# First quarter of the input projection as two parts of 256 rows, behind four condition loads instead of eight

## The reference

```python
mod = (jax.nn.silu(c) @ w_mod[l] + b_mod[l])[:, None, :]           # w_mod: 2048 x 12288
sa, ca, ga, sm, cm, gm = jnp.split(mod, 6, axis=-1)
mod_c = jax.nn.silu(c_ctx) @ w_mod[l] + b_mod[l]
sa_c, ca_c, ga_c, sm_c, cm_c, gm_c = jnp.split(mod_c, 6, axis=-1)
h_c = modulate(x_ctx, norm_attn_w[l], sa_c, ca_c)                  # rmsnorm(x, w) * (1 + scale) + shift
p_c_kv = h_c @ w_in[l][:, K_OFF:P_OFF]                             # keys and values of the context
h = modulate(x, norm_attn_w[l], sa, ca)
p = h @ w_in[l]                                                    # q, k, v, pool input u, gates
```

## Time and profile before

| | before |
|---|---|
| median of 3 runs | 2303.81 us |
| the profiled execution | 2304.4 us |
| its span | 2302.6 us |
| PE busy | 2264.9 us, 98% |
| first matmul of the projection | at 36.38 us |
| first matmul of the second quarter | at 126.13 us |
| DMA mean | 206 GB/s |

### The profile page before, as it was taken

The page is one execution under the profiler, slowest core; times in us unless marked ns, Lnnn a source line. Parts: engine busy times, 40 slices in busy tenths (PEclk is TensorE's granted clock), DMA queues, the critical chain, the costliest instruction groups (busy, mean ns, idle before and its releaser), DMA issues.

```text
span 2302.6 us, 30456 instructions
## 1 busy us (share of the span) xinstructions
PE 2264.9 (98%) x11865; PEld 1857.9 (81%) x11865; DVE 1551.5 (67%) x2297; ACT 1064.1 (46%) x1587; POOL 72.7 (3%) x91
## 2 busy tenths in 40 slices
PE   6999999999999999999999999999999999999998
PEld 3677787777888788888888888888987888899977
DVE  3577798777888776676655555754676545578875
ACT  4343234555544644344444443454554444466654
POOL 1100001110000100000000000000000000000000
PEclk8999999999999999999999999999999999999999
DMA  9999894444689677667655555555434566442233
GB/s 369 300 316 319 289 321 155 139 146 153 231 291 329 206 271 243 222 234 251 229 191 187 189 191 185 171 187 191 147 129 146 183 226 197 148 127 93 93 131 126
DMA packets 235011, 474.82 MB, mean 206 GB/s; under 512 B 7672, under 2 KB 10080, under 8 KB 233872
## 3 DMA queue, kind: packets, MB, share of 16 engines
q1 hardware_dynamic: 231280, 460.35, 59.5%
q0 software_dynamic: 3296, 12.74, 1.9%
q10 hardware_dynamic: 320, 0.13, 0.0%
HBM read 471.10 MB, written 2.10 MB: 206 GB/s over the span
## 4 chain that ended last, share of the span: by engine, by line
PE 96%; DMA 1%; DVE 1%; ACT 1%; issue 1%; SPq 0%; POOLq 0%; POOL 0%
PE acc L1884 75%; PE acc L2304 8%; PE acc L2346 2%; PE aux L2380 2%; PE turn L2360 2%; PE turn L1965 1%; PE aux L1917 1%; PE turn L2101 1%; DMA arena<-in_x 1%; DMA raw<-in_w_mod 1%; PE aux L2492 1%; PE acc L2116 1%; PE turn L2259 0%; DVE wlo L1083 0%; PE acc L2086 0%
## 5 line engine op out<-in xcount | busy, mean ns | idle before, releaser
L1083 DVE TENSOR_TENSOR wlo<-raw,whi 128x1024 fp32r<-128x1024 f32 x674 | 819.5, 1224 | 551.0 <-ACT whi L591 545.8
L591 ACT ACTIVATE whi<-raw 128x1024 fp32r<-128x1024 f32 x674 | 711.0, 1059 | 977.5 <-PE acc L1884 856.7
L1884 PE MATMUL acc<-whi,xhi 128*128 128x512 f32 x1536 | 425.4, 398 | 4.3 <-ACT xhi L673 2.6
L1884 PE MATMUL acc<-whi,xlo 128*128 128x512 f32 x1536 | 413.3, 390 | 0.5 <-DVE xlo L1483 0.5
L1884 PE MATMUL acc<-wlo,xhi 128*128 128x512 f32 x1536 | 412.5, 390 | 0.0
L1884 PEld LDWEIGHTS acc<-whi,xhi 128*128 128x128 f32 x1536 | 281.4, 188 | 86.5 <-issue 25.4
L1884 PEld LDWEIGHTS acc<-whi,xlo 128*128 128x128 f32 x1536 | 289.1, 188 | 62.8 <-DVE xlo L1483 1.0
L1884 PEld LDWEIGHTS acc<-wlo,xhi 128*128 128x128 f32 x1536 | 288.9, 188 | 61.2
L1884 PE MATMUL acc<-whi,hhi 128*128 128x512 f32 x512 | 139.7, 392 | 0.0
L1884 PE MATMUL acc<-whi,hlo 128*128 128x512 f32 x512 | 138.2, 389 | 0.0
L1884 PE MATMUL acc<-wlo,hhi 128*128 128x512 f32 x512 | 138.2, 389 | 0.0
(11 more groups left out here) (324 smaller groups left out, 2336.9 us busy)
## 6 DMA issues: line engine op xcount, KB each, us to landing
raw<-in_w_ff SPq DMA_DIRECT2D x128, 1024.0 KB, 5.2
raw<-in_w_mod SPq DMA_DIRECT2D x96, 1024.0 KB, 7.3
raw<-in_w_in SPq DMA_DIRECT2D x64, 1024.0 KB, 5.3
raw<-in_b_w_in SPq DMA_DIRECT2D x45, 1024.0 KB, 5.0
raw<-in_a_w_in SPq DMA_DIRECT2D x36, 1024.0 KB, 5.1
raw<-in_w_o SPq DMA_DIRECT2D x16, 1024.0 KB, 7.0
raw<-in_a_w_out SPq DMA_DIRECT2D x16, 1024.0 KB, 5.1
raw<-in_b_w_out SPq DMA_DIRECT2D x16, 1024.0 KB, 5.0
```

The source lines that it names most:

```text
L591: act.activation(whi[:, k % 2, on], raw[:, n % 4, on], ACT.Copy).then_inc(hi_ready, 1)
L1083: dve.tensor_tensor(wlo[:, k % 2, on], raw[:, LOAD_OF_UNIT[k] % 4, on], whi[:, k % 2, on].bitcast(F32), ALU.subtract)\
L1884: mm = pe.matmul(acc[:, bank0 + t, :], x[:, tile(kt), t * P:(t + 1) * P], w[:, u % 2, kk], start=kt == k_first and x is hi and w is whi, s ...
```

## The change

- The first quarter's 512 depth rows are taken as two parts of 256. A unit of it is 256 rows x 1024 columns, loaded as two DMAs of 512 KB, and gives two products of 12 matmuls with each of x and the context: 24 products of 12 matmuls in place of 12 of 24. The order is u, q, k, v for part 0 and then for part 1 (`FIRST`).
- The first product stands behind four conditions, each of which holds 256 columns of shift and 256 of scale (two DMAs, whose rows are 1 KB long instead of 2 KB). The second four follow behind the fourth unit. x is loaded ahead of the conditions.
- The context's squares are made half by ACT, half by DVE. `tables` moves from the end of the first quarter to behind its fourth unit.
- Conditions per quarter: 16, 8, 8, 0 in place of 18, 8, 6, 0. Sums per quarter: 0, 9, 9, 10 and one in each of heads 0 to 3, in place of 6, 8, 8, 10. The last of the eight `norm_column` stands in the up stage, with the scale and shift of the MLP. DVE's loop over heads 0 to 5 is written out.
- Seven parameter vectors are loaded into one partition and spread to all by one PE matmul with a row of ones; POOL loads 15 tensors first, and 4 later, these behind the first unit instead of the fourth.

```diff
-PHASES = [("front", 32, 48), ("att", 32, 8), ("up", 16, 8), ("wo", 16, 4),
+PHASES = [("front", 32, 60), ("att", 32, 8), ("up", 16, 8), ("wo", 16, 4),
...
-EARLY_CONDITIONS = {2: 2, 3: 2}
-FRONT_CONDITIONS = ((0, 4, 0, 1, 1, 1, 1, 2), (1, 1, 1, 1, 1, 1, 1, 1), (1, 1, 1, 1, 1, 1, 0, 0))
-COLUMNS_AT, LAST_COLUMNS_AT = 2, (7, 6, 6)
-FRONT_SUMS = ((0, 0, 2, 0, 0, 0, 2, 2), (0, 0, 2, 2, 0, 0, 2, 2), (0, 0, 2, 2, 0, 0, 2, 2), (1, 1, 2, 2, 1, 1, 2, 0))
+FIRST = [("u", 0), ("q", 0), ("k", 0), ("v", 0), ("u", 1), ("q", 1), ("k", 1), ("v", 1)]
+FIRST_PRODUCTS = [(u, rows, j) for u, (name, _) in enumerate(FIRST) for rows in range(2 if name in "kv" else 1) for j in range(2)]
+FIRST_CONDITIONS = {3: 4, 5: 2, 6: 2, 7: 2, 8: 2}
+FRONT_CONDITIONS = ((2, 2, 1, 1, 1, 1, 0, 0), (2, 2, 1, 1, 1, 1, 0, 0))
+COLUMNS_AT = 2
+FRONT_SUMS = ((1, 0, 2, 2, 0, 0, 2, 2), (1, 0, 2, 2, 0, 0, 2, 2), (1, 1, 2, 2, 1, 1, 2, 0))
 BY_BLOCK = [(b, rows) for b, (name, _) in enumerate(FRONT) for rows in range(2 if name in "kv" else 1)]
-FRONT_PRODUCTS = [[(0, 0), (1, 0), (2, 0), (3, 0), (2, 1), (3, 1)] + BY_BLOCK[6:]] + 3 * [BY_BLOCK]
 CONDITIONS1 = 8
-CONDITIONS_FIRST = 8
-CONDITIONS_AT = [n for quarter in FRONT_CONDITIONS for n in quarter]
+CONDITIONS_FIRST = 4
 SUM = {"norm": 0, "gates": 32, "mlp": 48}
-SUM_COLUMNS = {(0, 7): 0, (1, 3): 1, (1, 7): 2, (2, 3): 3, (2, 7): 4, (3, 2): 5, (3, 4): 6, (3, 7): 7}
+SUM_COLUMNS = {(1, 6): 0, (2, 1): 1, (2, 4): 2, (3, 0): 3, (3, 2): 4, (3, 5): 5, (3, 7): 6}
+FRONT_SUMMED = 28
...
+for _u, _n in FIRST_CONDITIONS.items():
+    LOADED_BEHIND[_u] += _n * ["mod"]
+for _u in range(7, 31):
+    LOADED_BEHIND[_u + 2] += (FRONT_CONDITIONS[_u // 8 - 1][_u % 8] if 8 <= _u < 24 else 0) * ["mod"]
+    LOADED_BEHIND[_u + 2] += FRONT_SUMS[(_u + 1) // 8 - 1][(_u + 1) % 8] * ["sum"]
+for _h in range(4):
+    LOADED_BEHIND[UNIT["att"] + 4 * _h + 2].append("sum")
...
+            if to is not None:
+                for part, x in enumerate(src):
+                    sp.dma_start(to(raw[:, n % 4], part), x.rearrange("(k p) n -> p k n", p=P)).then_inc(raw_in[n % 4], 16)
+                return
...
+            if b < 2:
+                both = [a["w_mod"][k * 512:(k + 1) * 512, s * D + b * 256:s * D + (b + 1) * 256] for s in range(2)]
+                load("mod", both, to=lambda x, s: x[:, :, s * 256:(s + 1) * 256])
+                return
...
+        sp.dma_start(res3, a["x"].rearrange("(t p) n -> p t n", p=P)).then_inc(rows_in, 16)
         for c in range(CONDITIONS_FIRST):
             load_condition()
-            if c == 3:
-                sp.dma_start(res3, a["x"].rearrange("(t p) n -> p t n", p=P)).then_inc(rows_in, 16)
-        for quarter in range(4):
+        for u, (name, part) in enumerate(FIRST):
+            c0 = FRONT_COLS[name]
+            load_unit([a["w_in"][part * 256:(part + 1) * 256, c0 + j * NW:c0 + (j + 1) * NW] for j in range(2)],
+                      to=lambda x, j: x[:, 2 * j:2 * j + 2])
+            if u == 1:
+                sp.dma_start(rows3, a["ctx"].rearrange("(t p) n -> p t n", p=P)).then_inc(ctx_in, 16)
...
-            (qkw[:, 0, :], a["q_norm_w"].partition_broadcast(P)), (qkw[:, 1, :], a["k_norm_w"].partition_broadcast(P)),
             (rcos, a["c_cos"]), (rsin, a["c_sin"]), (invf[:, 0, :], a["c_invf"]),
             (pos2[:, :], a["positions"].rearrange("(t p) -> p t", p=P)),
-            (sinks[:, :], a["sinks"].partition_broadcast(P)),
-        ] + [(lamv[:, n, :], a[f"lam{n}"].partition_broadcast(P)) for n in range(4)]
+        ]
...
-        pool.wait_ge(units_used, 2 * 4)
+        pool.wait_ge(units_used, 2)
...
+        act.activation(big[:, 2304:2688], turn[:, 1, 0:384], ACT.Copy)
+        act.activation(sinks[:, :], turn[:, 1, 384:416], ACT.Copy)
...
+        copy_front_condition(0)
+        split_halves(0, 1)
+        round_scaled()
+        split_halves(1, 3)
+        take_product(0)
+        take_product(1)
+        take_product(2)
+        take_product(3)
+        act.wait_ge(ctx_in, 16)
+        first_squares(T)
+        split(2, 1)
+        front_build(1)
+        split(3, 1)
+        for p in range(4, 10):
+            take_product(p)
         copy_front_condition(1)
-        split_halves(0, 1)
-        round_scaled(0)
-        round_scaled(1)
-        split_halves(1, 3)
-        for quarter in range(4):
+        take_product(10)
+        split(4, 1)
+        front_build(2)
+        take_product(11)
+        split(5, 1)
+        front_build(3)
+        split(6, 1)
+        split(7, 1)
+        copy_front_condition(2)
+        split(8, 1)
+        copy_front_condition(3)
+        for n in range(4, 6):
+            front_build(n)
+        split(9, 1)
...
+        take_first_condition(0)
+        scale_rows()
         front_build(0)
-        split_halves(0, 1)
+        split(0, 1)
+        scales(0, 2, 1)
+        split(1, 1)
+        dve.wait_ge(ctx_in, 16)
+        dve.wait_ge(sumsq_ready, 2)
+        dve.tensor_tensor_reduce(out=qkv[:, 4096:6144], in0=rows3[:, 1, :], in1=rows3[:, 1, :], scale=1.0, scalar=0.0, op0=ALU.mult,
+                                 op1=ALU.add, accum_out=lam[:, 7:8]).then_inc(sumsq_ready, 1)
+        first_mean(T)
+        first_norm(T)
+        split(2, 1)
         front_build(1)
-        scales(0, 1)
-        split_halves(1, 3)
-        for quarter in range(4):
+        split(3, 1)
+        tables()
+        take_first_condition(1)
+        scales(2, 2, 1)
+        split(4, 1)
+        front_build(2)
+        split(5, 1)
+        front_build(3)
+        for u, p in ((6, 12), (7, 14)):
+            for half in range(2):
+                add_product(p + half)
+                split_halves(2 * u + half, 1)
+        add_product(16)
+        add_product(17)
+        take_front_condition(2)
+        for half in range(2):
+            add_product(18 + half)
+            split_halves(16 + half, 1)
+        add_product(20)
+        add_product(21)
+        take_front_condition(3)
+        add_product(22)
+        for n in range(4, 6):
+            front_build(n)
+        split_halves(18, 1)
+        add_product(23)
+        split_halves(19, 1)
...
+            if h < 4:
+                sum_rows(total_of(c), SUM["norm"] + c, c % 4, (0, 1), None, norm_part if h == 3 else None)
...
+            if h < 4:
+                sum_rows(total_of(c), SUM["norm"] + c, c % 4, (2, 3))
...
-        with dve.Fori(0, HEADS1 - 2) as h:
-            end = looped(14, HEADS1 - 2)
-            head(h, h)
-            end()
-        head(HEADS1 - 2, None, squares=False)
-        head(HEADS1 - 1, None, squares=False, last=True)
+        for h in range(HEADS1):
+            head(h, squares=h < HEADS1 - 2, last=h == HEADS1 - 1)
...
+        pe.matmul(turn[:, 1, 0:416], sel[0:1, 0:P], param_row, start=True, stop=True).then_inc(setup_turned, 1)
+        pe.wait_ge(modw_ready, 2)
+        for c in range(3):
+            front_condition(c)
         pe.wait_ge(normed, T)
         pe.wait_ge(cols_ready, 2)
         front_rows(0)
-        front_rows(1)
-        front_columns(1)
-        next_condition, columns = 8, 2
-        for p, (quarter, (b, rows)) in enumerate((q, x) for q in range(4) for x in FRONT_PRODUCTS[q]):
-            shared, u = FRONT[b][0] in "kv", 8 * quarter + b
+        front_condition(3)
+        front_columns(0)
...
+            for x, w in ((hi, whi), (lo, whi), (hi, wlo)):
+                if w is wlo:
+                    pe.wait_ge(lo_ready, 2 * u + j + 1)
+                if x is lo:
+                    pe.wait_ge(xt_ready, built)
+                for kt in range(2):
+                    for t in range(T):
+                        mm = pe.matmul(acc[:, 2 * (p % 2) + t, :], x[:, 2 * part + kt, t * P:(t + 1) * P], w[:, u % 2, 2 * j + kt],
+                                       start=kt == 0 and x is hi and w is whi, stop=kt == 1 and w is wlo, skip_group_check=True)
+            mm.then_inc(shared_done if shared and rows == 0 else units_used, 1)
...
+        for p in range(5):
+            first_product(p)
+        pe.wait_ge(normed, 2 * T)
+        front_rows(1)
+        for p in range(5, 10):
+            first_product(p)
+        first_conditions(4, 4)
+        first_product(10)
+        front_columns(1)
+        front_rows(2)
+        first_product(11)
+        front_rows(3)
+        first_product(12)
+        first_product(13)
+        first_conditions(8, 2)
+        first_product(14)
+        first_product(15)
+        first_conditions(10, 2)
+        first_product(16)
+        first_product(17)
+        front_columns(2)
+        first_product(18)
+        first_product(19)
+        first_conditions(12, 2)
+        first_product(20)
+        first_conditions(14, 2)
+        first_product(21)
+        front_columns(3)
+        front_rows(4)
+        front_rows(5)
+        first_product(22)
+        first_product(23)```

```

(1 more changed line is left out.)

257 lines of the change are left out of this document (133 added, 124 removed).

## The result

The changed kernel takes 2310.71 us (median of 11 runs, 2309.3 to 2314.5), the kernel before 2304.98 beside it: ratio 1.0026, 95% interval 1.0017 to 1.0035. It is slower by 5.7 us, a little more than the 0.2% that I had called the limit of what can be told. The time lies inside the range of 2297 to 2312, near its upper end; the likeliest case (no change, 2305.3) was missed by 5.4. The profiled execution took 2309.57 us, a little less than the median; its span is 2307.8, 5.2 over that of before.

The account below looks back on a forecast made before the run. PE was taken as the bound, busy 2264.9 of 2302.6 us, so only idle time and work order could matter. Terms -5.0 + 2.8 + 3.7 = +1.5 us gave 2305.3 us, forecast as no change; range 2297 to 2312.

Parts of the forecast that it names:

- The start: Start of the projection's first product: forecast at 26.4 us, 10.0 us earlier than before.
- fourth condition lands at 20.7, incl. 0.7 for 1 KB rows: Loads ahead of the first product: six MB as before, landing at 20.7 us, with 0.7 added for shorter rows.
- three take 3.0: PE's first three conditions take 3.0 us, so the small loads have until 17 us and cost nothing.
- Squares of the context and product 4's copy: First quarter: ACT's late squares delay product 4 and its operand, 6.2 us; product 4's late copy delays product 6, 2.4.
- the wait for `wlo`: Product 4's last four matmuls wait for DVE's half behind the norm, 1.8 us; said to cover the low clock.
- The load of 15 us: Condition load beside POOL's small loads at 80 us: its 4.4 us wait and 1.8 at low clock were to go.
- Second part of the quarter: Later first quarter: waits of 0.6 at product 12, 0.9 at product 17, 0.5 at condition 15.
- T: Start of the second quarter's first product: 126.13 us before, forecast 121.1, which is 5.0 earlier.
- The doubled conditions: Quarters 2 and 3: paired conditions wait for late slots, 2.1, 1.1 and 0.5 us, in sum 3.7.
- The heads: Heads 0 to 3: the added sums on DVE are covered by slack, cost 0; without cover 6 us in all.
- The sum: Whole kernel: -5.0 at the second quarter's start, +2.8 work moved behind it, +3.7 doubled conditions, giving +1.5 us.
- The slower rival: Slots in quarters 2 and 3 fall behind (8 for 3.7) and heads lose 4: +9.8, 2313.6 us, chance 0.25.

Follow-up runs that it names:

- e9: Changed kernel with early context squares and identity turns in PE's waits, first eight conditions loaded as whole 2 KB-row tiles (wrong columns, timing only): 2299.28 us.
- e1: Changed kernel with the first product's first condition put ahead of PE's turns of the small parameters: 2310.96 us.
- e2: Changed kernel with ACT's context squares right behind the copy of product 0 and its splits between the later copies: 2301.52 us.
- e4: Kernel before with only the parameter spread: seven small parameters loaded as rows and spread by PE instead of seven broadcast loads: 2299.10 us.
- e3: Changed kernel with the kernel before's order of conditions, 18 ahead of the second quarter and none doubled: 2313.05 us.
- e12: Changed kernel with early context squares and identity turns in PE's waits, plus single conditions and one sum ahead, as in the kernel before's load order: 2296.84 us.

## Why the prediction was right or wrong

*The start: 26.4 forecast, 27.78 measured.* The term "fourth condition lands at 20.7, incl. 0.7 for 1 KB rows" is mis-sized: landing 21.6 to 22.0, and the rows cost 1.0 to 1.5 (e9). The Trainium skill (DMA: Bandwidth & Descriptors, Specifications) would have had no loss from 512 bytes on; here 1 KB rows ran at 348 GB/s and 2 KB rows at 387. The rest is "three take 3.0": they took 5.28, from 16.37 to 21.65, with a turn of 0.6 behind it. The small loads themselves had landed at 14.05, well ahead of the 17 that I had allowed them. What I had left out is the 2.3 us of turns and the spreading matmul behind them and the slow matmuls at the start; in the kernel before, too, the first 24 take 4.52. Moving the small loads out of the way by itself gives nothing (e1), since the landing and the clock still hold.

*Squares of the context and product 4's copy.* The mechanism was right, as was its place (product 4 at 44.5, forecast 43.5; product 6 at 55.7, forecast 53.5). The idle time was 4.0, 0.8 and 1.2 in place of 4.4, 1.8 and 2.4, but the low clock took more than the difference back: products 4 and 5 and the turn between them took 9.2 us of work where I had 6.0. The Trainium skill (TensorE: Matmul & The Clock Gate, Part 1) has the clock halve when TensorE has been idle; the trace agrees, with 0.57 on the mean from 44.5 to 52 behind 4 us without work. I had held this to be covered by the wait for `wlo`, and it was not. The whole is 9.2 by the timeline (5.9 idle, 3.3 clock) and 8.0 by e2, in the forecast 8.6 (6.2 + 2.4). That the sum fits is partly luck: the idle time was 2.7 too high and the clock was at nothing.

*The load of 15 us.* Right in cause and size: forecast 4.4 + 1.8 = 6.2, e4 gives 5.9. Whether it is the copies or the place of the seven loads was not tried apart.

*Second part of the quarter.* 0.6, 0.9 and 0.5 were 0.2, 0.3 and 0.4.

T was forecast at 121.1 and measured at 123.38. Of the 2.3 between them 1.4 is the start, 0.6 the squares (9.2 for 8.6) and -1.1 the second part (0.9 for 2.0). The rest, 1.3, is PE's own work from product 6 on: 66.8 us where the forecast has 65.5.

*The doubled conditions: 3.7 forecast, 5.5 measured. This is the other mis-sized term.* In the second quarter the first pair is right in place, chain and size (1.84 at 131.8 for 2.1; slot free at T + 3.3, forecast T + 3.5), but the second pair waits 0.96 where I had nothing. In the third quarter both conditions of the first pair wait, 0.84 and 1.47 for 1.1, and the second pair 0.40 for 0.5. I had followed the pairs one by one and taken the ring behind each to be in step. Nor is the doubling alone the cause, as I had written: undone by itself it gained nothing (e3). The order of the tiles in the ring decides: a sum is a tile whose slot comes free without PE, and the change took the sums out of the places behind the first units of the quarter. With conditions and one sum back in their places 2.8 are left (e12).

*The heads.* Cost 0 forecast; from 365 us on the kernel keeps its distance of 4.2 until the added norm column. Right.

*The sum.* -5.0 + 2.8 + 3.7 = +1.5 became -2.75 + 2.8 + 5.51 = +5.6 (5.2 in the spans). Both misses, 2.3 in T and 1.8 in the ring, go the same way. The slower rival named ring and heads with 9.8: its ring was to cost 4.3 more than the forecast and cost 1.8 more; of its heads nothing came true.
